# Fourth tile of x turned over DRAM, the first latents' norm ahead of the eighth tile's turn, three q copies ahead of the seventh latents

## The reference

```python
h = rmsnorm(x, norm_mix[l])
proj = jnp.einsum('bsd,dc->bsc', h, w_in[l])
qa, ka, va, ga, cq, ckv, kr, gb = jnp.split(proj, split_idx, axis=-1)
ya = window_attention(qa, ka, va, attn_sink[l]) * silu(ga)      # group A, shapes left out
q  = jnp.einsum('bsc,ce->bse', rmsnorm(cq, q_a_norm[l]), w_uq[l])
kv = jnp.einsum('bsc,ce->bse', rmsnorm(ckv, kv_a_norm[l]), w_ukv[l])
yb = latent_attention(q_nope, q_rope, k_nope, k_rope, v_b) * silu(gb)
x  = x + jnp.einsum('bsc,cd->bsd', jnp.concatenate([ya, yb], -1), w_out[l])
return rmsnorm(x, final_norm)
```

## Time and profile before

| | us |
|---|---|
| median of 3 runs | 604.65 |
| the runs | 604.17 to 606.27 |
| the profiled execution's own time | 605.02 |
| its span (what the trace shows) | 603.2 |
| TensorE busy in the span | 594.0 (98%) |
| DVE busy | 445.0 (74%) |
| ACT busy | 355.7 (59%) |
| POOL busy | 294.4 (49%) |

### The profile page before, as it was taken

One profiled execution on the slowest core, in us unless ns is written; L12 is line 12 of the kernel. 1 busy time (PEld: TensorE's weight loads), 2 busy tenths in 40 slices (PEclk: granted clock), 3 DMA queues, 4 the chain that ended last, 5 costly groups with the idle time before them and its releaser, 6 DMA issues.

```text
span 603.2 us, 9190 instructions
## 1 busy us (share of the span) xinstructions
PE 594.0 (98%) x3068; PEld 483.1 (80%) x3068; DVE 445.0 (74%) x806; ACT 355.7 (59%) x762; POOL 294.4 (49%) x273
## 2 busy tenths in 40 slices
PE   8999999999999999999999999999999999999996
PEld 7888887888888888888887777777777777878885
DVE  5777563334434439989999788998998988799684
ACT  6645123213333238777886678888888888524563
POOL 4610702515756432535547536786786776420701
PEclk9999999999999999999999999999999999999998
DMA  7688459684776620101005966777768745599043
GB/s 254 187 282 227 132 146 283 208 285 131 263 255 232 204 69 2 36 1 36 2 27 116 252 158 179 197 179 194 194 173 196 195 121 180 161 383 349 1 164 117
DMA packets 74911, 102.11 MB, mean 169 GB/s; under 512 B 13416, under 2 KB 45680, under 8 KB 74864
## 3 DMA queue, kind: packets, MB, share of 16 engines
q1 hardware_dynamic: 74704, 101.25, 56.1%
q10 hardware_dynamic: 160, 0.27, 0.1%
HBM read 60.17 MB, written 31.62 MB: 152 GB/s over the span
## 4 chain that ended last, share of the span: by engine, by line
PE 78%; DMA 6%; DVE 6%; ACT 4%; SPq 2%; POOL 2%; issue 2%; ACTq 0%; POOLq 0%; DVEq 0%
PE ps L1910 14%; PE ps L1912 14%; PE ps L1911 14%; PE ps L2203 8%; PE ps L2181 7%; PE ps L2111 5%; PE ps L2116 5%; PE ps L2081 3%; PE ps L2131 2%; PE ps L2091 2%; DMA lat<-lat_scratch 2%; DMA lat_scratch<-lat_b 2%; PE ps L2068 2%; PE ps L2067 2%; PE ps L2092 2%
## 5 line engine op out<-in xcount | busy, mean ns | idle before, releaser
L1760 DVE TENSOR_TENSOR pT_lo<-ps,pT_hi 128x512 fp32r<-128x512 f32 x102 | 69.2, 684 | 21.7 <-ACT pT_hi L1285 20.8
L1910 PE MATMUL ps<-hT_hi,w_hi 128*128 128x512 f32 x208 | 84.0, 404 | 0.0
L1912 PE MATMUL ps<-hT_hi,w_lo 128*128 128x512 f32 x208 | 81.4, 391 | 0.0
L1911 PE MATMUL ps<-hT_lo,w_hi 128*128 128x512 f32 x208 | 81.1, 390 | 0.0
L1272 ACT ACTIVATE p_b<-ps,stat 128x1024 f32<-128x1024 f32 x64 | 71.3, 1114 | 12.5 <-DVE stat L1735 12.0
L1735 DVE TENSOR_REDUCE stat<-ps 128x1 f32<-128x1024 f32 x64 | 76.5, 1212 | 2.2 <-PE ps L2131 2.0
L1285 ACT ACTIVATE pT_hi<-ps 128x512 fp32r<-128x512 f32 x102 | 60.3, 596 | 23.4 <-PE ps L2181 23.1
L2181 PEld LDWEIGHTS ps<-ident,p_b 128*128 128x128 f32 x408 | 48.7, 140 | 17.7 <-issue 5.2
L2181 PE MATMUL ps<-ident,p_b 128*128 128x128 f32 x408 | 62.0, 275 | 0.6 <-DVE pT_lo L1760 0.3
L823 POOL TENSOR_SCALAR p_w<-p_w,stat 128x384 f32<-128x384 f32 (+1 forms) x40 | 24.4, 623 | 55.3 <-DVE stat L1643 55.3
L939 POOL TENSOR_TENSOR pT_lo<-p_land,pT_hi 128x512 fp32r<-128x512 f32 x26 | 33.4, 1290 | 30.6 <-ACT pT_hi L1292 30.6
(11 more groups left out here) (241 smaller groups left out, 1503.4 us busy)
## 6 DMA issues: line engine op xcount, KB each, us to landing
w_raw<-w_in SPq DMA_DIRECT2D x13, 512.0 KB, 4.2
probs_scratch<-p_blk SPq DMA_DIRECT2D x52, 128.0 KB, 2.8
p_land<-probs_scratch SPq DMA_DIRECT2D x13, 512.0 KB, 4.8
x_in<-x SPq DMA_DIRECT2D x8, 512.0 KB, 3.9
wt_raw<-w_out SPq DMA_DIRECT2D x8, 512.0 KB, 4.4
t_scratch<-wt_hi SPq DMA_DIRECT2D x16, 256.0 KB, 2.7
t_scratch<-wt_lo SPq DMA_DIRECT2D x16, 256.0 KB, 2.9
q<-q_h SPq DMA_DIRECT2D x16, 256.0 KB, 3.6
```

Of the source, the lines that this page charges most:

```text
L1760: nc.vector.tensor_tensor(pT_lo[at_], ps[:, 4 + a, :].rearrange("p (k c) -> p k c", c=P), f(pT_hi[at_]), ALU.subtract).then_inc(s_bTl, 1)
L1910: nc.tensor.matmul(o, a_hi, b_hi, start=first, stop=False, skip_group_check=goes_on)
L1911: nc.tensor.matmul(o, a_hi, b_lo, start=False, stop=False, skip_group_check=goes_on)
L1912: return nc.tensor.matmul(o, a_lo, b_hi, start=False, stop=last, skip_group_check=goes_on)
```

## The change

Three things are done.

1. `X_PE` becomes 3: tile 3 is turned over DRAM like tiles 4 to 7. TensorE's `turn_x(3)` goes away; DVE gets a `turn_blocks(3)`; SP gets a `store_x(3)` (four DMAs) and a `fetch_x(3)`, which lands in the last row of `latT_hi`. `x_blk` number 0 moves to 201 KB, where `lat` isn't touched. The tiles now alternate buffers with tile 3 in number 1. On SP the loads of `g_q` and `g_kv` stand behind the load of tile 6, and `fetch_x(4)` ahead of `store_x(5)`. The split of tile 3 stands later: `h_hi(3)` behind `square_x(6)` on ACT and `h_lo(3)` behind `norm_x(6)` on DVE.
2. On DVE `lat_norm(0)` and `h_lo(4)` stand between `norm_x(7)` and `turn_blocks(7)`, where they stood behind `turn_blocks(7)`. `lat_norm(0)` no longer waits for a store.
3. On ACT `lat_hi(6)` stands behind the copies of the q jobs 0, 1 and 2, where it stood ahead of them.

The diff, without its repetitions:

```diff
@@ -62,7 +62,7 @@
 BASE = 16512
-X_PE = 4
+X_PE = 3
 ACT_UNITS = range(2, 16, 2)
@@ -124,7 +124,7 @@
 
-        x_blk = [at(f"x_blk{i}", kb, [P, 4, KT, Q32]) for i, kb in enumerate((147, 161))]
+        x_blk = [at(f"x_blk{i}", kb, [P, 4, KT, Q32]) for i, kb in enumerate((201, 161))]
 
@@ -236,7 +236,7 @@
         s_wnh, s_wnr = sem("wn_hi_ready"), sem("wn_ready")
-        s_grow, s_gcol, s_gT, s_gb = sem("g_row_in"), sem("g_col_ready"), sem("g_turned"), sem("g_broadcast")
+        s_grow, s_gcol, s_gT, s_gb = sem("g_row_then_fourth_tile_in"), sem("g_col_ready"), sem("g_turned"), sem("g_broadcast")
         s_pA, s_pB = sem("natA_done"), sem("natB_done")
@@ -390,7 +390,9 @@
 
-            a, r = ((latT_hi, 0), (latT_hi, 2), (latT_lo, 0), (latT_lo, 2))[t - X_PE]
+            if t == X_PE:
+                return f(latT_hi[:, 4, :]).rearrange("p (r c) -> p r c", r=2)
+            a, r = ((latT_hi, 0), (latT_hi, 2), (latT_lo, 0), (latT_lo, 2))[t - X_PE - 1]
             return f(a[:, r:r + 2, HALF:SEQ])
@@ -436,8 +438,7 @@
             load_wn(7)
-            sp.dma_start(g_q[:, :], q_a_norm.partition_broadcast(P)).then_inc(s_glat, 16)
-            sp.dma_start(g_kv[:, :], kv_a_norm.partition_broadcast(P)).then_inc(s_glat, 16)
+
             def store_x(t):
@@ -448,13 +449,17 @@
                 sp.dma_start(x_turned(t), xt_scr[t - X_PE].rearrange("a p (r q) c -> (a p) r (q c)", r=2)) \
-                    .then_inc(s_xq[t - X_PE], 16)
-
+                    .then_inc(s_xq[t - X_PE - 1] if t > X_PE else s_grow, 16)
+
+            store_x(3)
             load_x(6)
+            sp.dma_start(g_q[:, :], q_a_norm.partition_broadcast(P)).then_inc(s_glat, 16)
+            sp.dma_start(g_kv[:, :], kv_a_norm.partition_broadcast(P)).then_inc(s_glat, 16)
+            fetch_x(3)
             store_x(4)
             load_x(7)
+            fetch_x(4)
             store_x(5)
-            fetch_x(4)
             store_x(6)
@@ -1011,7 +1016,7 @@
                 if t >= X_PE:
-                    act.wait_ge(s_xq[t - X_PE], 16)
+                    act.wait_ge(s_xq[t - X_PE - 1], 16) if t > X_PE else act.wait_ge(s_grow, 32)
                     for r in range(2):
@@ -1127,11 +1132,11 @@
             square_x(4)
-            h_hi(3)
             wn_hi_k(6)
...
             square_x(6)
+            h_hi(3)
             square_x(7)
@@ -1142,10 +1147,11 @@
             last_stats()
-            lat_hi(NT - 2)
 
...
             for j, (kind, t, h) in enumerate(UP):
+                if j == 3:
+                    lat_hi(NT - 2)
                 if j == 4:
@@ -1467,8 +1473,8 @@
                     dve.wait_ge(s_latT, t - 1)
-                else:
-                    dve.wait_ge(s_xsto[t], 128)
+                elif t == 1:
+                    dve.wait_ge(s_xsto[1], 192)
                 dve.wait_ge(s_lrms, t + 1)
@@ -1523,10 +1529,9 @@
             h_lo(0, range(1, 2))
-            for t in range(1, 4):
+            for t in range(1, X_PE):
                 norm_x(t)
-                if t < 3:
-                    h_lo(t)
+                h_lo(t)
             def turn_blocks(t):
@@ -1536,11 +1541,12 @@
                 norm_x(t)
+                if t == 6:
+                    h_lo(3)
+                if t == 7:
+                    lat_norm(0)
+                    h_lo(4)
                 turn_blocks(t)
-                if t == 4:
-                    h_lo(3)
-            lat_norm(0)
-            h_lo(4)
 
@@ -1976,7 +1982,6 @@
             both(2, range(4))
-            turn_x(3)
             for k in (4, 5):
```

## The result

| | before | after |
|---|---|---|
| median | 605.13 | 609.79 |
| the runs | 604.17 to 606.27 | 607.21 to 610.84 |
| profiled execution | 605.02 | 607.97 |
| its span | 603.2 | 606.2 |

The ratio is 1.0073, with a 95% interval from 1.0058 to 1.0088: the changed kernel is slower by 0.7%. By the ratio that is 4.4 us, and the two medians lie 4.66 apart. The forecast was 606.8 with a range up to 608.8, so the direction was right and the size was not.

The account below looks back on a forecast made before the run. TensorE's work and the latents' rounds were taken to bound the kernel, meeting at job 6. By the latents, 91.73 + 3.6 + 2.38 = 97.71 instead of 95.57: +2.1 on 604.65 gives 606.8 us, range 604.0 to 608.8.

Parts of the forecast that it names:

- The transposes' 0.79: Eight transposes of tile 3 leave TensorE at 24.93, freeing 0.79 us, part of the 1.32 us that is the most to gain.
- the 0.53 of job 6: TensorE's lost time ahead of the first matmul of job 6 in the kernel before, 0.53 us.
- TensorE's own arrival: When job 6 could start if only TensorE's work counted: 94.81 + 0.23 - 0.79 = 94.25.
- The rival of the late tile: Tile 3's low part ends 1.5 us beyond 37.4, delaying tile 7's turn and the latents: 608.3 us, chance 0.14.
- the upper bound of 4.5: Largest delay taken for the first latents' store, with tile 7's load 1.2 us later still.
- both paths: First latents' store behind tile 7's stores on SP (+3.35); second latents' norm waiting for those stores to land (+4.1).
- S: Delay of the latents' rounds, taken to reach the seventh latents' landing whole: 3.6 us, between 3.35 and 4.1.
- the copies: Three ACT copies run before the seventh latents land: -1.46 us, leaving 2.38 from landing to job 6.
- the first round: First pass of the latents over DRAM, beginning with the first latents' store: 48.2 instead of 44.85, 3.35 us later.
- the rounds: Repeated store, fetch, high part, low part, norm and turn of the latents, without slack, from 44.85 on.
- Behind job 6 everything follows TensorE: After job 6 TensorE has no long wait, so the end moves by the same 2.1 us: 606.8.
- The clock falls: Rival: after 3.5 us of idle TensorE one q job runs at 1.2 GHz, 2.07 us more: 608.9 us, chance 0.08.

Follow-up runs that it names:

- norm_first: Kernel before with one edit in VectorE's order: first latents' norm and low part of tile 4 ahead of the turn of tile 7; median 609.72 us.
- swap: Changed kernel with the first latents' store ahead of tile 7's four stores on SP; median 608.28 us.
- latb1: Changed kernel with the second latents' block buffer moved from 161 KB, shared with tile 7, to 202.5 KB; median 610.36 us.
- tile3_only: Changed kernel without its second part, with g_q and g_kv loaded behind tile 7's load and tile 5's stores ahead of tile 4's fetch; median 604.87 us.
- turn7: Changed kernel with VectorE's order put back as before and SP's changed order left; median 608.31 us.
- no_copies: Changed kernel without its third part: the seventh latents' high part stands ahead of the three copies again; median 610.82 us.
- spin28: Changed kernel with 28 unread transposes of the identity ahead of job 6, keeping TensorE busy in the wait; median 607.98 us.
- split: Changed kernel with the 1152 KB load of w_uq cut in three of 384 KB, the later two behind latents' fetches; median 607.79 us.
- traffic: Kernel before plus one more tile's DRAM traffic that no engine reads, 512 KB loaded and four stores of 128 KB; median 606.83 us.

## Why the prediction was right in kind and wrong in size

**What TensorE gives.** The transposes' 0.79 and the 0.53 of job 6 were no gain, as said; the wait swallowed them. TensorE's own arrival was forecast for 94.25 and was 94.69 + 0.23 = 94.92. Of the 0.67, 0.39 are there from 7.75 us on, where the same transposes had started at 7.36, and 0.28 come at 33.9 us, at the low part of the last `wn` slice, for which the prediction had allowed some tenths.

**Tile 3.** Its low part ended at 38.5 instead of 37.4, and TensorE had no wait for it. The rival of the late tile fell.

**Tile 7 and the first latents.** The load was issued at 33.79 (forecast 33.0), and the norm of tile 7 ended at 42.4 (41.2). `norm_x(4)` met GpSimd's `wn_lo` as forecast, with 2.45 where 1.42 stood; `norm_x(5)` took 2.46, but it had taken 2.45 in the kernel before too. It ended 1.11 later, within the forecast's 0 to 1.3. What the prediction left out is that SP was then busy with the stores of tile 4, up to 33.74, so the load was 1.67 late and not 0.9, and that the load took 5.4 us to land instead of 4.9. So the first latents' store came at 49.28 instead of 48.2: +4.43 against the +3.35, by the upper bound of 4.5. The second norm's reciprocal was 51.26 for 50.8. The mechanism, VectorE's turn of tile 7 behind the norm and both paths behind that turn, is shown to be enough by norm_first, by swap and latb1 (either path alone is enough), and by tile3_only (with the turn in its old place and SP's order mended the loss is gone). It is not needed for the delay: there is a second hold of nearly the same length in SP's order, tile 5's stores behind tile 4's fetch, which the prediction did not see. turn7 shows it: with VectorE's order put back the turn comes at 45.32 for 46.21, and the first latents' store stays at 49.25 for 49.28. In the changed kernel it is hidden behind VectorE's order.

**S and the copies.** The seventh latents landed at 95.50 (forecast 95.3), so S was 3.77 for 3.6, and the 4.43 of the first round had shrunk by 0.66. From the landing to job 6 it took 2.37 us (2.38). Job 6 started at 97.87 (97.7). This half of the sum was right to 0.2 us. Some of that is luck: tile 7 was 1.2 us later than forecast, the rounds gave 0.66 back, and a hold that the sum does not have would have put the store in the same place.

**The step that failed** is the last one: "Behind job 6 everything follows TensorE, which has no long wait, so the end moves by the same 2.1". In the profiled execution the start of latent attention moved by 3.89. Of this, 2.30 are job 6. The other 1.59 are TensorE's own work at a granted clock of 0.50, 1.2 GHz, between 1.5 and 4.5 us behind the wait: the distance to the kernel before grows from 2.35 to 3.87 between 99.38 and 102.73 and then stands. The rival "The clock falls" had this, with a price of 2.07 us and a time of 608.9, and it was given a chance of 0.08 because the rows of before showed a clock of 1.00 beside a wait of 0.53. That is no evidence on a wait of 3.5, as the text itself said; 0.08 was far too low, and the range left most of the case out. The Trainium skill, TensorE: Matmul & The Clock Gate, section HAM oscillation, has it that work behind a long enough idle stretch starts at half rate. The rows agree in the size, 0.43 for 0.23, and only in part in the place: in no_copies and norm_first the work behind the wait starts at half rate, while in the changed kernel it starts at 0.23 and falls 1.5 us later, and in swap it does not fall at all.

The profiled execution (607.97) was one of the lighter cases, and by itself it lies inside the range of the forecast; the median does not. Its granted clock over the span was 0.996; the six runs of the changed kernel lie along their clocks, from 607.21 at 0.997 over 609.46 at 0.995 to 610.84 at 0.992, and 0.005 of a span of 606 is 3.0 us. That these are longer stretches behind the same wait fits no_copies, whose 0.50 lasts from about 98 to 104, but in an execution without a profile the place of the fall isn't seen, so it is an inference. If job 6 is as late in every execution as in the profiled one, the 4.7 us of the medians are made of 2.3 for job 6 and some 2.4 for the clock. spin28 divides them otherwise, 1.8 for the clock and 3.4 for the rest, and the runs don't decide between the two.

**What stays open.** The runs at a clock of 0.997 to 0.999 also scatter, by 4 us in tile3_only (603.86 to 607.79), and by as much in split. What sets that is not known. One of the 75 runs of the kernel before that were taken beside the experiments had a clock of 0.993 and took 609.40, without any edit; all others had 0.997 or more. And whether the clock falls after a wait of 2 to 3 us is not decided by its length here: swap lost 3.03 us and split 2.33 without a fall in their profiles, traffic 2.05 with one.

## What to carry to other kernels

When an instruction is moved ahead of another to get its result out sooner, look at the queue that carries the result: if what it overtook feeds the same queue ahead of it, the result waits there for the thing overtaken, and everything behind it as well. Where two chains meet at an engine within some tenths of a microsecond, work taken from one gains nothing, and a delay of the other can be paid twice: once as the wait, and once, in some executions (here at stops of 2.05 us and more), as work at half clock behind it. An early transfer in a stage whose queue is nearly full has a price, here 1.7 to 2.3 us at the end of the rounds for 1 MB (tile3_only and traffic), and it is paid where something waits for a transfer beside it. And a mechanism that explains the delay to 0.2 us need not be the only one that holds it: put back the one edit, and see whether the delay goes.

## What the runs showed of the hardware

- The granted clock fell to about 0.50 around stops of TensorE of 2.05 to 5.7 us at job 6 or at tile 4, and in none of the profiles around a stop of 1 us or less there. Of the profiles with a stop from 2.3 to 3.1 us two showed no fall (swap, split). The fall can come 1.5 us after the work has started again (99.4 in the changed kernel) as well as during the stop (between 96 and 98 in no_copies). With 28 small transposes that nobody reads in the wait (spin28) it stood at 1.00 in the profile.
- Four products of 128x80 on VectorE took 0.66 us alone and 2.54 beside GpSimd's subtractions, and a norm of two 128x512 1.42 and 2.45. The Trainium skill, GPSIMD Engine Reference, section Specifications, says that GpSimd shares its SBUF interfaces with VectorE, with contention for VectorE instructions with two SBUF inputs. The rows agree, and the four short ones were stretched more (3.8 times against 1.7).
